# Projecting columns before their norm is known, with the inputs in four pieces, at the head of a two-block transformer kernel

## What is computed

```python
u = x * rsqrt(mean(x * x, -1) + 1e-6) * norm_mix_g      # rms norm over 1024 channels
proj = u @ w_in        # split into qa, ka, va, qb, ckv, krope, qi, ki, wi, gates ga, gb
```

## Time and profile before

| | |
|---|---|
| median of 3 runs | 2841.2 us (2840.55 to 2850.65) |
| the profiled execution | 2835.44 us |
| its span in the trace | 2833.7 us (1.7 us lie around it) |
| mean granted TensorE clock | 0.944 of full speed |
| TensorE busy | 89% of the span |

### The profile page before, as it was taken

The page is one execution under the profiler, slowest core; times in us unless marked ns, Lnnn a source line. Parts: engine busy times, 40 slices in busy tenths (PEclk is TensorE's granted clock), DMA queues, the critical chain, the costliest instruction groups (busy, mean ns, idle before and its releaser), DMA issues.

```text
span 2833.7 us, 35724 instructions
## 1 busy us (share of the span) xinstructions
PE 2531.1 (89%) x14507; PEld 1948.4 (69%) x14507; DVE 1529.5 (54%) x3252; ACT 839.1 (30%) x1455; POOL 799.0 (28%) x754
## 2 busy tenths in 40 slices
PE   5999998899878787869989977799999999999998
PEld 5685544467644444447765566699999999988887
DVE  3136656553200000024634999889978888864443
ACT  2124322142100000023432237733333333333332
POOL 0002200000100000010001149745555666634442
PEclk8999999999999999969999987899999999999999
DMA  8326300024899999961104005799999999989995
GB/s 317 126 90 242 119 30 30 30 92 198 335 423 420 422 422 420 423 223 60 60 30 186 31 27 182 255 388 353 357 384 360 385 371 379 382 333 352 347 358 202
DMA packets 154905, 718.50 MB, mean 254 GB/s; under 512 B 16424, under 2 KB 31568, under 8 KB 125552
## 3 DMA queue, kind: packets, MB, share of 16 engines
q1 hardware_dynamic: 91904, 490.15, 44.0%
q0 software_dynamic: 62832, 226.00, 20.9%
HBM read 658.54 MB, written 57.16 MB: 253 GB/s over the span
## 4 chain that ended last, share of the span: by engine, by line
PE 62%; DVE 20%; DMA 11%; ACT 3%; issue 2%; POOL 1%; SPq 0%; POOLq 0%; DVEq 0%; ACTq 0%
PE psum L3329 10%; PE psum L3316 9%; DMA arena<-w 8%; PE psum L1615 5%; PE psum L430 4%; PE psum L2681 4%; PE psum L2145 4%; DVE arena L3467 3%; PE psum L3277 3%; DVE rounded L3416 3%; PE psum L946 2%; PE psum L1622 2%; DMA arena<-v_rows,arena 2%; PE psum L1219 2%; PE psum L1234 2%
## 5 line engine op out<-in xcount | busy, mean ns | idle before, releaser
L3329 PEld LDWEIGHTS psum<-rounded,rounded 128*128 128x128 f32 x3072 | 453.1, 189 | 31.8 <-issue 22.3
L3329 PE MATMUL psum<-rounded,rounded 128*128 128x320 f32 x3072 | 464.3, 311 | 6.8 <-DVE rounded L3416 4.6
L3316 PEld LDWEIGHTS psum<-rounded,rounded 128*128 128x128 f32 x2880 | 424.2, 188 | 21.8 <-ACT rounded L3399 10.9
L3316 PE MATMUL psum<-rounded,rounded 128*128 128x320 f32 x2880 | 432.5, 311 | 2.4 <-DVE rounded L3416 2.4
L3264 POOL DMA_INDIRECT arena<-u_rows,arena x192 | 281.8, 1468 | 245.0 <-DVE arena L3467 151.6
L1615 PE MATMUL psum<-arena 128*64 128x256 f32 x2048 | 259.6, 417 | 79.0 <-issue 52.8
L3354 ACT ACTIVATE rounded<-arena 128x1024 fp32r<-128x1024 f32 x248 | 256.5, 1050 | 243.1 <-PE psum L3329 203.0
L3416 DVE TENSOR_TENSOR rounded<-arena,rounded 128x1024 fp32r<-128x1024 f32 x248 | 302.5, 1220 | 15.6 <-ACT rounded L3354 15.6
L1615 PEld LDWEIGHTS psum<-arena 128*64 128x64 f32 x2048 | 182.6, 151 | 167.7 <-issue 118.6
L3264 POOL DMA_INDIRECT arena<-v_rows,arena x192 | 230.9, 1203 | 220.9 <-PE psum L3277 147.3
L1738 DVE COPY arena<-psum 128x256 f32<-128x256 f32 x32 | 13.6, 424 | 442.5 <-PE psum L1665 442.5
(11 more groups left out here) (457 smaller groups left out, 3431.6 us busy)
## 6 DMA issues: line engine op xcount, KB each, us to landing
arena<-w SPq DMA_DIRECT2D x96, 2048.0 KB, 27.4
arena<-v SPq DMA_DIRECT2D x64, 1024.0 KB, 8.0
arena<-uT SPq DMA_DIRECT2D x60, 1024.0 KB, 8.3
arena<-wada SPq DMA_DIRECT2D x12, 2048.0 KB, 8.1
arena<-wp SPq DMA_DIRECT2D x10, 2048.0 KB, 10.1
arena<-gd SPq DMA_DIRECT2D x30, 640.0 KB, 7.0
xb<-arena SPq DMA_DIRECT2D x1, 12032.0 KB, 42.4
gd<-arena SPq DMA_DIRECT2D x11, 1024.0 KB, 11.8
```

The lines of the kernel that those rows point to most:

```text
L3316: ins = pe.matmul(PS[:, b, 0:DT], w[:, x, k, :], hv[:, y, :], k == 0 and i == 0, k == 7 and i == 2)
L3329: ins = pe.matmul(PS[:, b, 0:DT], w[:, y, x, :], gg[:, z, :], x == 0 and i == 0, x == 7 and i == 2)
```

## The change

Projections run on `x * gain`, not yet divided by the rms; the factor per token is multiplied in when a bank is emptied. Squares go to 8 buffers (`SQ`) that lie elsewhere, the sums go to banks 6 and 7, and `RN` (the factors) gets a place of its own that stays until the last chunk is emptied. The host lays the meta columns out as 128x8x16; they land in `MT` and GpSimd copies them into XT.

```diff
-    SQ = at3(o_qi, 4, TK)
-    RN = at(OW, TK)
+    SQ = at3(O_TEMP + 8 * TK, 8, TK)
+    RN = at(2 * RING + 3 * 2112 + T + TK, TK)
+    MT = at3(OW + 3 * TK, 8, META)
...
     def inputs_sp(sp):
-        sp.dma_start(out=XT[:, :, 0:META], in_=A["metaT"].rearrange("(k p) t -> p k t", p=128)).then_inc(*d_in())
-        sp.dma_start(out=XT[:, :, META:TK], in_=A["xT"].rearrange("(k p) t -> p k t", p=128)).then_inc(*d_in())
+        sp.dma_start(out=MT, in_=A["metaT"]).then_inc(*d_gain())
+        sp.dma_start(out=VEC, in_=A["vec"]).then_inc(*d_gain())
+        xt = A["xT"].rearrange("(k p) t -> p k t", p=128)
+        for i in range(4):
+            sp.dma_start(out=XT[:, 2 * i:2 * i + 2, META:TK], in_=xt[:, 2 * i:2 * i + 2, :]).then_inc(*d_columns[i]("x", i))
         sp.dma_start(out=CST, in_=A["cst"]).then_inc(*d_in())
-        sp.dma_start(out=VEC, in_=A["vec"]).then_inc(*d_in())
+        for p in (0, 1):
+            fetch(sp, p, p * RING, A["wp1"][p], "wp1", p)
         sp.dma_start(out=COS, in_=A["cos"]).then_inc(*d_tab())
...
         sp.dma_start(out=WUV, in_=A["wuv"]).then_inc(*d_tab())
-        for p in (0, 1):
-            fetch(sp, p, p * RING, A["wp1"][p], "wp1", p)
+
+    def zeros_sp(sp):
         sp.wait_ge(*N1.dv["zero"])
...
     def norm1_pe(pe):
         pe.wait_ge(*d_in.end())
-        norm_pe(pe, N1, SQ, TK, 0)
+        for k in range(8):
+            pe.wait_ge(*(N1.dv if k % 2 else N1.ac)["square", k])
+            for i, (a, w) in enumerate(FULL):
+                pe.matmul(PS[:, 6 + i, 0:w], ONE, SQ[:, k, a:a + w], k == 0, k == 7).then_inc(*N1.pe("sum", k, i))
 
     def norm1_ac(ac):
+        gain = vec_gain(V_MIX)
+        ac.preload_act_table_set("silu_and_others")
+        ac.wait_ge(*d_gain.end())
+        ac.activation(SC8, VEC[:, V_COND:V_COND + 8], ACT.Silu).then_inc(*N1.ac("cond"))
+        ac.wait_ge(*N1.po["meta"])
+        for k in (0, 2, 4, 6):
+            ac.wait_ge(*d_columns[k // 2]["x", k // 2])
+            ac.activation(SQ[:, k, :], XT[:, k, :], ACT.Square).then_inc(*N1.ac("square", k))
+        for k in range(8):
+            ac.activation(u_part(k, 0), XT[:, k, :], ACT.Copy, scale=gain(k)).then_inc(*N1.ac("upper", k))
         ac.wait_ge(*d_in.end())
...
     def norm1_dv(dv):
+        gain = vec_gain(V_MIX)
+        dv.memset(ZERO, 0.0).then_inc(*N1.dv("zero"))
+        dv.wait_ge(*N1.po["meta"])
+        for k in (1, 3, 5, 7):
+            dv.wait_ge(*d_columns[k // 2]["x", k // 2])
+            dv.tensor_tensor(SQ[:, k, :], XT[:, k, :], XT[:, k, :], ALU.mult).then_inc(*N1.dv("square", k))
+        for k in range(8):
+            dv.wait_ge(*N1.ac["upper", k])
+            dv.scalar_tensor_tensor(u_part(k, 1), XT[:, k, :], gain(k), u_part(k, 0).bitcast(F32), ALU.mult, ALU.subtract).then_inc(
+                *N1.dv("lower", k))
         dv.wait_ge(*d_in.end())
...
+    def mean_dv(dv):
+        dv.wait_ge(*N1.pe["sum", 7, 1])
+        for i, (a, w) in enumerate(FULL):
+            dv.tensor_scalar(RN[:, a:a + w], PS[:, 6 + i, 0:w], 1.0 / 1024, EPS, ALU.mult, ALU.add).then_inc(
+                *(N1.dv("mean") if i else N1.dv()))
+        dv.wait_ge(*N1.ac["root"])
+        dv.reciprocal(RN, RN).then_inc(*N1.dv("scale"))
+        dv.wait_ge(*N1.dv["scale"])
+
+    def normed_dv(dv, k):
+        dv.scalar_tensor_tensor(UT[:, k, :], XT[:, k, :], vec_gain(V_MIX)(k), RN, ALU.mult, ALU.mult).then_inc(*N1.dv("out", k))
+
+    def root_ac(ac):
+        ac.wait_ge(*N1.dv["mean"])
+        ac.activation(RN, RN, ACT.Sqrt).then_inc(*N1.ac("root"))
 
     def norm1_po(po):
+        po.wait_ge(*d_gain.end())
+        po.tensor_copy(XT[:, :, 0:META], MT).then_inc(*N1.po("meta"))
         po.wait_ge(*d_in.end())
...
     def proj_sp(sp):
         for p, free in ((2, P.dv["split", 3]), (3, P.dv["split", 7]), (4, P.pe["vm"])):
+            if p == 4:
+                zeros_sp(sp)
             sp.wait_ge(*free)
             fetch(sp, p % 2, (p % 2) * RING, A["wp1"][p], "wp1", p)
...
     def proj_pe(pe):
...
-                    pe.wait_ge(*P.dv["ut", k // 2])
+                    pe.wait_ge(*N1.dv["lower", k])
...
-        pe.wait_ge(*N1.dv["out", 7])
+        bank[6] = bank[7] = N1.dv["mean"]
         for j in range(4):
             project(j, 2 * j, FULL, 0)
-            bank[2 * j] = bank[2 * j + 1] = (P.dv if j % 2 else P.ac)["ka", j]
+            bank[2 * j] = bank[2 * j + 1] = P.dv["ka", j]
...
         w = ring2(2)
+        pe.wait_ge(*N1.dv["out", 7])
...
     def proj_ac(ac):
...
-        ac.wait_ge(*N1.dv["out", 7])
-        for k in range(4):
-            ac.activation(parts(UTR[k], 2)[:, 0], UT[:, 2 * k:2 * k + 2, :], ACT.Copy).then_inc(*P.ac("ut", k))
-        for j in range(4):
+        ahead(0)
+        root_ac(ac)
+        for j in range(8):
             ahead(j)
...
     def proj_dv(dv):
...
+        RX = RN[:, META:TK]
+        ahead(0)
+        mean_dv(dv)
         for j in range(4):
             ahead(j)
-            if j % 2:
-                dv.wait_ge(*P.pe["chunk", j])
-                dv.tensor_copy(pair(KA[:, j, :]), PS[:, 2 * j:2 * j + 2, 0:264]).then_inc(*P.dv("ka", j))
+            dv.wait_ge(*P.pe["chunk", j])
+            dv.tensor_tensor(pair(KA[:, j, :]), PS[:, 2 * j:2 * j + 2, 0:264], pair(RN), ALU.mult).then_inc(*P.dv("ka", j))
+            normed_dv(dv, 2 * j)
+            normed_dv(dv, 2 * j + 1)
         for j in range(4):
             ahead(4 + j)
-            if j % 2:
-                dv.wait_ge(*P.pe["chunk", 4 + j])
-                dv.tensor_scalar(QA[:, j, :], PS[:, j, :], 0.125, None, ALU.mult).then_inc(*P.dv("qa", j))
+            dv.wait_ge(*P.pe["chunk", 4 + j])
+            dv.scalar_tensor_tensor(QA[:, j, :], PS[:, j, :], 0.125, RX, ALU.mult, ALU.mult).then_inc(*P.dv("qa", j))
...
+        ahead(12)
+        dv.wait_ge(*P.pe["chunk", 12])
+        dv.scalar_tensor_tensor(RB, PS[:, 0, :], 0.125, RX, ALU.mult, ALU.mult).then_inc(*P.dv("rb raw"))
...
         for j in range(4):
             ahead(17 + j)
...
+            dv.tensor_tensor(QI[:, j, :], PS[:, 3 + j, :], RX, ALU.mult).then_inc(*P.dv("qi", j))
             if j == 1:
                 dv.wait_ge(*N1.ac["cond"])
                 sums(dv, 8)
-                dv.wait_ge(*P.pe["chunk", 19])
+            if j == 2:
                 dv.tensor_copy(VM2, VM).then_inc(*P.dv("vm2"))
```

More of the change, by code:

```diff
@@ L266, in build @@
     yb = nc.dram_tensor("yb", [ROWS, 1024], F32, kind="Internal").ap()
-    d_in, d_tab, d_zero, d_rot = (dma_counter(x) for x in ("in", "tables", "zero", "rotated"))
+    d_in, d_tab, d_zero, d_rot, d_gain = (dma_counter(x) for x in ("in", "tables", "zero", "rotated", "gains"))
+    d_columns = [dma_counter(f"columns{i}") for i in range(4)]
     ring = [dma_counter(f"ring{i}") for i in range(9)]
@@ L299, in inputs_sp @@
                          in_=ZERO[0:2 * ROWS - 128 * nz, :]).then_inc(*d_zero())
[L302 to L335, removed]
@@ L337, in vec_gain, with u_part @@
     def vec_gain(col):
         return lambda k: VEC[:, col + k:col + k + 1]
-    N1 = Stage(counter, "norm1", "pe ac dv")
+    N1 = Stage(counter, "norm1", "pe ac dv po")
+    UTR = [alias(2 * RING + 2112 * i, 2112) for i in range(3)] + [alias(o_kmb + 2048, 2112)]
+    assert o_kmb + 2048 + 2112 <= O_XT
+    def u_part(k, x):
+        return parts(UTR[k // 2], 2)[:, x, k % 2, :]
     def norm1_pe(pe):
         pe.wait_ge(*d_in.end())
-        norm_pe(pe, N1, SQ, TK, 0)
+        for k in range(8):
+            pe.wait_ge(*(N1.dv if k % 2 else N1.ac)["square", k])
+            for i, (a, w) in enumerate(FULL):
+                pe.matmul(PS[:, 6 + i, 0:w], ONE, SQ[:, k, a:a + w], k == 0, k == 7).then_inc(*N1.pe("sum", k, i))
@@ L371, in build @@
     RK = at(2 * RING + 3 * 2112 + T, TK)
-    assert 2 * RING + 3 * 2112 + T + TK <= 4 * RING
+    assert 2 * RING + 3 * 2112 + T + 2 * TK <= 4 * RING
     def ring2(p):
@@ L456, in proj_pe @@
             project(8 + j, 1 + j, XONLY, META)
-            bank[1 + j] = (P.dv if j % 2 else P.ac)["qbn", j]
+            bank[1 + j] = P.dv["qbn", j]
         def swapped(x, name, bs, m, hs, src):
@@ L486, in proj_pe @@
         project(16, 6, XONLY, META)
-        bank[6] = P.ac["ri raw"]
-        pe.wait_ge(*P.ac["kin"])
+        bank[6] = P.dv["ri raw"]
+        pe.wait_ge(*P.dv["kin"])
         claim(2, 3, 4, 5)
@@ L508, in proj_pe @@
             project(17 + j, 3 + j, XONLY, META)
-            bank[3 + j] = (P.dv if j % 2 else P.ac)["qi", j]
+            bank[3 + j] = P.dv["qi", j]
         claim(7)
@@ L537, in ahead @@
                 ac.activation(parts(WSP1[i % 3], 8)[:, 0], raw, ACT.Copy).then_inc(*P.ac("split", i))
-        def pair(x):
-            return x.rearrange("p (a b) -> p a b", a=2)
-        ac.wait_ge(*N1.dv["out", 7])
-        for k in range(4):
-            ac.activation(parts(UTR[k], 2)[:, 0], UT[:, 2 * k:2 * k + 2, :], ACT.Copy).then_inc(*P.ac("ut", k))
-        for j in range(4):
-            ahead(j)
-            if j % 2 == 0:
```

(13 more changed lines are left out.)

81 lines of the change are left out of this document (24 added, 57 removed).

## The result

The changed kernel takes 2818.74 us (median of 4 runs, 2812.29 to 2823.11) against 2841.64 us before (4 runs, 2840.55 to 2850.65): a ratio of 0.9915, 95% interval 0.9892 to 0.9939, some 24 us (the two medians lie 22.9 us apart). The profiled execution took 2823.11 us, its span is 2821.1 us, the mean granted clock 0.946.

What follows compares the result with a forecast made beforehand. Bound: a chain of waits holding TensorE up to 41.6 us. Chunk 0 starting earlier (20.3 us) plus clock (2.3) makes 22.6 off 2841.2: 2818.6 us, own range 2812 to 2826, range with two rivals 2808 to 2832.

Steps and rivals of the forecast that it cites:

- The chain of waits as the bound: Up to 41.6 us one file of steps holds TensorE: 17.8 us of norm tail, plus 2.33 us lost to low clock.
- the first rival: The clock stays low for chunks 0 to 2: gain only 13.6 us, time 2827.6 us; chance 0.07.
- Path one: The sums ahead of chunk 0: CST lands at 11.4 us, sums take 9.7, so chunk 0 starts at 21.3.
- Path two: Split 0 ahead of chunk 0: weight piece 0 lands at 18.2 us with tables behind it; split ready at 20.6.
- Clock: Without the 17.8 us gap behind the sums, chunk 0 runs at full clock in 5.85 us: 2.3 us more gained.
- New load on VectorE, cost nothing: Evacuations, rotations and splits per chunk take VectorE 3.3 of 5.85 us, 4.0 of 5.9 in chunks 13 to 15: no cost.
- The fills: Moved on SP behind weight piece 3, done at 97.5 us; piece 4 issued at 103.0, slack 8.5 us.
- The sum: 20.3 us from the earlier start of chunk 0 plus 2.3 us of clock: 22.6 us gained.
- VectorE was in no wait of TensorE: Rival: VectorE, late with evacuations and splits, gives back 13 us; gain 9, time 2832 us; chance 0.07.
- the fills did not block piece 4: Rival: at 0.2 MB/us the fills end at 144.4 us, weight piece 4 is 38.4 late; time 2857 us; chance 0.03.
- The play of 4 us among runs: Some 4 us of spread among runs of the whole kernel, allowed for in the forecast's own range, 2812 to 2826 us.

Runs made afterwards that it cites:

- old inputs: The changed kernel with inputs in the old order, x in one transfer and weights behind the tables; 2822.54 us, ratio 0.9926 to the kernel before.
- weights first: "ones and UR" plus weight piece 0 ahead of the rest of CST, engines waiting for that rest only after split 2; 2817.56 us, ratio 0.9912.
- inputs alone: The kernel before with VEC first, x in four pieces and two weight pieces ahead of the tables, norm as before; 2837.6 us, ratio 0.9988.
- wait for UT: The changed kernel with UT made in one go after the reciprocal and chunk 0 waiting for all of it; 2833.52 us, ratio 0.9975 to before.
- wait for the reciprocal: The changed kernel with a wait put back, so chunk 0 waits for the reciprocal; 2823.7 us, ratio 0.9954 to the kernel before.
- fills first: The changed kernel with the fills issued right behind the tables, at about 8 us; 2824.81 us, ratio 0.9949 to the kernel before.
- emptied twice: The changed kernel with each of the 21 chunks emptied and multiplied twice into the same place on VectorE; 2820.23 us, ratio 0.9935 to before.
- ones and UR: The changed kernel with the matrix of ones as its own transfer ahead of x, and UR copied before va 3 is emptied; 2818.96 us, ratio 0.9914.

## Why the prediction was right, step by step

- **The chain of waits as the bound**, 17.8 us of norm behind the sums and 2.33 us of low clock: right. Gap and clock were both put back by an experiment and both came back at vm. One sentence under the first rival is right for the head only: that the clock fell only after TensorE had stood idle. In the same trace of before it is also at 0.50 from 186.1 to 193.0 us, with TensorE busy in every record (last section).
- **Path one**: CST landed at 3.74 + 8.04 = 11.78 us (said 11.4), sums 9.62 (9.7), first projection 21.44 (21.3). The slow first records are there again, 6 in 2 us and later 11:

```profile
13.80:15.80 2.00, 2.00 (x6) 1.59 (x5) 1.00 1.02 434
17.80:19.80 2.00, 2.00 (x11) 1.71 (x10) 1.00 1.01 434
```

- **Path two**: piece 0 was there at 4.52 + 12.1 = 16.6 us, not 18.2, split 0 at 19.2, not 20.6. The term took off 2.6 us for the tables alone, and 4.2 were gained. With the new layout of the meta columns but the old order ("old inputs") the piece landed at 5.55 + 14.7 = 20.25, 0.6 before the 20.8 of the kernel before, so the new order brought 3.6; what makes up the 1 us beyond the tables stays open. None of it was on the path. The rate in these rows is 434 GB/s, and 415 over the whole stretch of the sums, so the figure of 358 that the prediction takes from the Trainium skill, page "DMA: Bandwidth & Descriptors", section Specifications, is again not what the trace shows. The same row of that table works it out as 716 GB/s shared by two cores; one core ran here.
- **Clock**: chunk 0 took 5.9 us (said 5.85).
- **New load on VectorE, cost nothing**: right, and with as much again it is still nothing.
- **The fills**: piece 4 was issued at 103.14 (said 103.0) and the split that reads it was released by TensorE, as said. But the cover was mis-sized. I had the queue empty at 97.5; the large fill landed at 53.68 + 48.9 = 102.6, 0.5 us before piece 4 was issued. The 44.9 us counted all bytes at 409 GB/s from the issue of piece 3 on. The queue moved 290 GB/s in the first ten of these (52.8 to 62.9 us; piece 3 took 10.0 us to land, where its bytes at that rate are 5), some 409 up to 90 us, and 345 in the last 12.6: 2.9 and 2.0 us of the 5 that are missing. The slack is some 3.5 us, not 8.5, and an earlier vm eats it up: in "weights first" the large fill landed at 99.98 us, 0.9 behind the issue of piece 4. The split that reads piece 4 was still released by TensorE, at 110.26.
- **The sum**: 22.6 forecast, 22.5 measured at vm, 22.9 between the medians. The forecast of the time, 2818.6 against 2818.74, is closer than the measurement allows: the same kernel's medians in two other series were 2825.09 and 2822.56 us.
- **The rivals**: the clock did not stay low, VectorE was in no wait of TensorE, and the fills did not block piece 4. The play of 4 us among runs was set too small: one stage alone differs by 10 between two executions of the kernel before. That the median came out within 0.2 us of the forecast is luck; that 22.5 us were gained at vm is not.

All kernels together, vm's end in the trace against the ratio to before:

| kernel | vm ends, us | earlier than 125.6 | 1 - ratio, x 2841 us |
|---|---|---|---|
| inputs alone | 123.8 | 1.8 | 3 (-3 to 10) |
| wait for UT | 117.5 | 8.1 | 7 (1 to 14) |
| wait for the reciprocal | 110.6 | 15.0 | 13 (8 to 19) |
| fills first | 110.2 | 15.4 | 14 (8 to 20) |
| old inputs | 105.2 | 20.4 | 21 (13 to 29) |
| emptied twice | 103.3 | 22.3 | 18 (12 to 25) |
| the changed kernel, second series | 103.7 | 21.9 | 20 (12 to 28) |
| the changed kernel, first series | 103.1 | 22.5 | 24 (17 to 31) |
| the changed kernel, third series | 102.9 | 22.7 | 22 (15 to 29) |
| ones and UR | 101.4 | 24.2 | 24 (18 to 31) |
| weights first | 99.1 | 26.5 | 25 (18 to 32) |

What is gained at the head arrives at the end, within the interval in each case. No later step is seen to give it back; with intervals of 7 us to either side, one that gave back a few us would not be seen.

## What to carry to other kernels

A factor that belongs to a column can be multiplied in when the bank is emptied, which takes the whole tail of a norm out of the start of the matmuls; price the gap together with the clock, since 5.4 us of idling cost 8.4 here, 3.0 of it in the low clock of the chunks behind it, and a gap of 3.6 us was followed by 1.8 us of such loss and one of 2.2 by next to none, in one profile each. When a stage is pulled forward, look at every transfer that used to be harmless: the two fills would have taken back 7.1 of the 22.5 us had they kept their place in the queue's order. Read the gain at a landmark next to the change, in both traces, because one later stage differed by 10 us between two executions of one kernel. And take more than one profile: two that agree within 1 us can still share one of several lengths.

## What was not expected

- **When the clock falls is not fixed by the length of the gap.** In two profiles of the same kernel before, the sums end at 23.84 us in both; the granted clock falls at 29.1 us in one and at 25.9 in the other. Over all kernels with a gap behind the sums it fell 2.0 to 5.3 us after the last sum, in "ones and UR" after the gap was over. So that it fell with a gap of 3.6 us and held with one of 2.2 is one execution each, and no rule. What decides was not tried.
- **The clock also falls without a gap.** One row each for the same 64 matmuls of 8 columns (the product for `wi`), in the two profiles of the kernel before:

```profile
180.60 8.83 PE L499 MATMUL psum<-arena 128*128 128x8 f32 x64
```

```profile
180.67 11.84 PE L499 MATMUL psum<-arena 128*128 128x8 f32 x64
```

TensorE is busy in every record up to them, the clock falls while they run, at 186.1 us in the first and at 182.9 in the second, and it is back at 1.00 at 193.0 and 196.5. From the end of vm to "meta later" the kernels take 100.0, 101.6 or 103.2 us, each of the thirteen profiles one of the three within 0.1, kernels with and without the change alike. So a gain read at that later landmark is uncertain by 3 us, at vm by less than 1.
- **The stage from 205 to 590 us takes one of a few lengths, 14 us apart at most.** The same 1131 matmul records took 371.1 to 384.8 us over the thirteen profiles, with a mean granted clock of 0.95 in the short ones and 0.92 in the longest, and profiles of different kernels share their low stretches. That these stretches and the length go together is seen in the rows; which of the two drives the other, and what picks one set of stretches, stays open. The time at which the stage starts does not pick it alone: it starts at 204.7 us in the changed kernel and at 228.9 in the second profile of before, with the same set.
